# A C table of eight positions in two parts, lag zero as its own products, and added masked scores in a two-layer encoder

## The reference

```python
# S5: a diagonal state-space model, 32 groups of 16 channels, 64 complex states, both directions
bu = einsum('gpc,blgc->blgp', b_bar, u)
states = associative_scan(a_r * a_l, a_r * b_l + b_r)        # over the sequence, forward or reverse
y = einsum('gcp,blgp->blgc', c, states).real                 # summed over both directions, + d * u
...
# GLA: gated linear attention in chunks of 64, four heads, both directions
scores = where(causal_in_chunk, einsum('bnihd,bnjhd->bnhij', q_rel, k_rel), 0.0)
o_intra = einsum('bnhij,bnjhe->bnihe', scores, v)
o_inter = einsum('bnihd,bnhde->bnihe', q * exp(bcum), S_prev)
o = o_intra + o_inter                                        # summed over both directions
```

## Time and profile before

| | |
|---|---|
| time, median of 3 runs | 2458.53 us (2458.19 to 2458.97) |
| the profiled execution | 2458.74 us, of which the span (first to last instruction) is 2457.0 us |
| PE busy | 2420.5 us, 99% |
| DVE busy | 1518.9 us, 62% |
| ACT busy | 1156.1 us, 47% |
| granted TensorE clock, mean | 0.999 of full speed |

### The profile page before, as it was taken

The page is one execution under the profiler, slowest core; times in us unless marked ns, Lnnn a source line. Parts: engine busy times, 40 slices in busy tenths (PEclk is TensorE's granted clock), DMA queues, the critical chain, the costliest instruction groups (busy, mean ns, idle before and its releaser), DMA issues.

```text
span 2457.0 us, 35475 instructions
## 1 busy us (share of the span) xinstructions
PE 2420.5 (99%) x14201; PEld 2065.3 (84%) x14201; DVE 1518.9 (62%) x2570; ACT 1156.1 (47%) x2034; POOL 0.2 (0%) x4
## 2 busy tenths in 40 slices
PE   9999999999999999999999999999999999999999
PEld 5888776778898999898788888888888898888887
DVE  8898757676466755674665447858885554533333
ACT  4333445364444645654453445736764443523432
POOL 0000000000000000000000000000000000000000
PEclk9999999999999999999999999999999999999999
DMA  5435642274223555444224324223234423433232
GB/s 193 107 75 138 218 138 65 78 238 146 86 76 105 181 182 171 120 130 128 78 73 160 112 86 123 92 86 107 92 95 143 132 78 99 133 99 99 95 96 93
DMA packets 110723, 291.34 MB, mean 119 GB/s; under 512 B 18944, under 2 KB 41600, under 8 KB 109280
## 3 DMA queue, kind: packets, MB, share of 16 engines
q1 hardware_dynamic: 99088, 260.38, 33.9%
q10 hardware_dynamic: 11472, 28.71, 3.6%
HBM read 267.45 MB, written 19.50 MB: 117 GB/s over the span
## 4 chain that ended last, share of the span: by engine, by line
PE 82%; DVE 5%; ACT 1%; issue 1%; ACTq 0%; DVEq 0%
PE ps L1455 70%; PE ps L1568 2%; PE ps L1525 2%; PE ps L1550 2%; PE ps L1592 1%; DVE wlo L1432 1%; PE ps L1581 1%; PE ps L1982 1%; DVE ringP L1824 0%; PE ps L1538 0%; PE ps L1992 0%; PE ps L1599 0%; PE ps L1929 0%; PE ps L1469 0%; DVE ps L1748 0%
## 5 line engine op out<-in xcount | busy, mean ns | idle before, releaser
L1427 ACT ACTIVATE whi<-wraw 128x1024 fp32r<-128x1024 f32 x430 | 452.1, 1052 | 188.7 <-PE ps L1455 128.4
L1455 PE MATMUL ps<-in_hP,whi 128*128 128x512 f32 x1336 | 532.5, 399 | 1.6 <-issue 1.6
L1432 DVE TENSOR_TENSOR wlo<-wraw,whi 128x1024 fp32r<-128x1024 f32 x430 | 522.8, 1218 | 3.1 <-ACT whi L1427 2.8
L1455 PE MATMUL ps<-in_hP,wlo 128*128 128x512 f32 x1336 | 520.9, 390 | 0.0
L1455 PE MATMUL ps<-in_lP,whi 128*128 128x512 f32 x1336 | 520.1, 389 | 0.0
L1455 PE MATMUL ps<-in_hS,whi 128*128 128x256 f32 x1088 | 318.0, 292 | 5.6 <-DVE x L1770 4.3
L1455 PE MATMUL ps<-in_lS,whi 128*128 128x256 f32 x1088 | 309.1, 284 | 0.0
L1455 PE MATMUL ps<-in_hS,wlo 128*128 128x256 f32 x1088 | 308.9, 284 | 0.0
L1455 PEld LDWEIGHTS ps<-in_hP,whi 128*128 128x128 f32 x1336 | 250.9, 188 | 59.6 <-issue 8.9
L1455 PEld LDWEIGHTS ps<-in_hP,wlo 128*128 128x128 f32 x1336 | 250.8, 188 | 53.5
L1455 PEld LDWEIGHTS ps<-in_lP,whi 128*128 128x128 f32 x1336 | 251.1, 188 | 51.8 <-issue 1.4
(11 more groups left out here) (486 smaller groups left out, 3671.7 us busy)
## 6 DMA issues: line engine op xcount, KB each, us to landing
wraw<-wt SPq DMA_DIRECT2D x432, 512.0 KB, 3.6
wraw<-wt ACTq DMA_DIRECT2D x17, 512.0 KB, 4.3
k_scratch<-region_P SPq DMA_DIRECT2D x16, 256.0 KB, 3.1
v_scratch<-vtmp SPq DMA_DIRECT2D x32, 128.0 KB, 3.0
x<-x_in SPq DMA_DIRECT2D x4, 768.0 KB, 7.1
mix_mem<-mem_in ACTq DMA_DIRECT2D x1, 2048.0 KB, 15.7
x<-x_in ACTq DMA_DIRECT2D x1, 2048.0 KB, 12.8
region_S<-k_scratch ACTq DMA_DIRECT2D x2, 1024.0 KB, 5.4
```

Of the source, the lines that this page charges most:

```text
L1427: nc.scalar.activation(whi[:, (n + 3) % NHI, :, :], wraw[:, ws(n), :, :], ACT.Copy).then_inc(wh.sem, 1)
L1432: nc.vector.tensor_tensor(wlo[:, ws(n), :, :], wraw[:, ws(n), :, :], whi[:, (n + 3) % NHI, :, :].bitcast(F32), ALU.subtract).then_inc(wr.s ...
L1455: last = nc.tensor.matmul(ps[:, m % 2, 0:N[prod.g]], w_[:, k, :], x_[:, k, :], start=(k == 0 and j == 0), stop=(k == KT - 1 and j == 2))
```

## The change

- `cl` and `qf` have eight positions (lags 1 to 8 for forward, 8 to 1 for reverse) in place of ten. `dve_cl` works on all eight groups at a time, in two parts, real and imaginary: the real part where the first half was, the imaginary part where the second was.
- `pe_lag` makes seven lags (112 columns) per group and direction and places them by group in four column parts of the array (output partitions 0, 32, 64, 96), two groups side by side in a bank: banks 4 and 6. Lag 0 of both directions together is a product of its own: `bbar` by `cc` and by `cneg`, the negated imaginary part (one new DVE instruction, once), 128 rows, 16 columns, into bank 5.
- `act_rt` is eight copies of 16x224 in place of two, and `dve_rt` four additions of 16x32 in place of two of 16x128.
- `pe_bu` waits for each part of `vT` by itself, and writes part 0 to banks 6 and 7, part 1 to 4 and 5.
- In the last block `load_chunks` of group 1 comes after `act_rt` and `load_mt` and before group 2; before, it came ahead of `act_rt`.
- `pe_zeros`, products that nothing reads at the very start, are 33 of 512 columns instead of 25 of 512 and 10 of 256.
- `dve_masks` also adds the two masked scores of a head (two additions per unit), and `pe_heads` multiplies the sum once, for all j first, and then the states. DVE no longer waits there for the unit before.

```diff
-POS = SC + 2
+LAGS = (SC - 1) * GC
...
-                for i in range(15):
-                    nc.tensor.matmul(ps[:, 7, :], w_, x_, start=(i == 0), stop=(i == 14))
-                for i in range(10):
-                    nc.tensor.matmul(ps[:, 6, :], w_, x_, start=(i == 0), stop=False, skip_group_check=True)
-                    nc.tensor.matmul(ps[:, 6, 0:TS], w_, x_[:, 0:TS], start=False, stop=(i == 9), skip_group_check=True)
+                for i in range(33):
+                    nc.tensor.matmul(ps[:, 7, :], w_, x_, start=(i == 0), stop=(i == 32))
...
             def pe_lag(pe, b):
                 pe.wait_ge(cl_ready.sem, b + 1)
                 pe.wait_ge(vt_ready.sem, 2 * b + 2)
-                for g in range(GB):
-                    for z in range(2):
-                        rows = slice(NS * z, NS * z + NS)
-                        lo = 0 if z == 0 else 2
-                        for i in range(2):
-                            last = nc.tensor.matmul(banks(4 + 2 * z, 1024)[0:GC, g * P:(g + 1) * P], bbar[rows, i, GB * b + g, :],
-                                                    cl[rows, i, g, lo:lo + SC, :].rearrange("p n c -> p (n c)"),
+                for e in range(2):
+                    for i in range(2):
+                        for q in range(4):
+                            g = 2 * q + e
+                            for z in range(2):
+                                rows = slice(NS * z, NS * z + NS)
+                                nc.tensor.matmul(ps[32 * q:32 * q + GC, 4 + 2 * z, e * LAGS:(e + 1) * LAGS], bbar[rows, i, GB * b + g, :],
+                                                 cl[rows, i, g, z:z + SC - 1, :].rearrange("p n c -> p (n c)"), start=(i == 0), stop=(i == 1))
+                for e in range(2):
+                    for i, c_ in enumerate((cc[:, 0], cneg)):
+                        for q in range(4):
+                            h = GB * b + 2 * q + e
+                            last = nc.tensor.matmul(ps[32 * q:32 * q + GC, 5, e * GC:(e + 1) * GC], bbar[:, i, h, :], c_[:, h, :],
                                                     start=(i == 0), stop=(i == 1))
                 last.then_inc(lag_done.sem, 1)
...
-                else:
-                    pe.wait_ge(vt_ready.sem, 2 * b + 2)
                 for i in range(2):
+                    pe.wait_ge(vt_ready.sem, 2 * b + i + 1)
                     for g in range(GB):
-                        o = banks(4 + 2 * i, 1024)[:, g * P:g * P + NCH]
+                        o = banks(6 - 2 * i, 1024)[:, g * P:g * P + NCH]
...
-                nc.scalar.activation(rt[:, :, SC:LAG, :], lagf[:, :, 1:SC, :], ACT.Copy)
-                nc.scalar.activation(rt[:, :, 0:SC, :], lagb, ACT.Copy).then_inc(rt_copied.sem, 1)
+                for q in range(4):
+                    nc.scalar.activation(rt[:, 2 * q:2 * q + 2, 0:SC - 1, :], lagb[q], ACT.Copy)
+                    last = nc.scalar.activation(rt[:, 2 * q:2 * q + 2, SC:LAG, :], lagf[q], ACT.Copy)
+                last.then_inc(rt_copied.sem, 1)
...
-            def dve_cl(v, b, halves=(0, 1)):
+            def dve_cl(v, b, parts=(0, 1)):
...
+                for i in parts:
+                    nc.vector.tensor_tensor(cl[:, i], cb[0], qb[i], ALU.mult)
+                    dve_chain(nc.vector.tensor_tensor(tmp, cb[1], qb[1 - i], ALU.mult))
+                    last = nc.vector.tensor_tensor(cl[:, i], cl[:, i], tmp, ALU.subtract if i else ALU.add)
...
             def dve_rt(v, b):
                 v.wait_ge(rt_copied.sem, b + 1)
-                dve_chain(nc.vector.tensor_tensor(rt[:, :, SC - 1, :], rt[:, :, SC - 1, :], lagf[:, :, 0, :], ALU.add))
-                nc.vector.tensor_tensor(rt[:, :, SC - 1, :], rt[:, :, SC - 1, :], dd[:, GB * b:GB * b + GB, :], ALU.add)\
-                    .then_inc(rt_ready.sem, 1)
+                for q in range(4):
+                    last = nc.vector.tensor_tensor(rt[:, 2 * q:2 * q + 2, SC - 1, :], dd[:, GB * b + 2 * q:GB * b + 2 * q + 2, :], lag0[q], ALU.add)
+                last.then_inc(rt_ready.sem, 1)
...
                         tile(t2)
-                        if b == NB - 1:
-                            a.wait_ge(cl_ready.sem, NB)
-                            load_chunks(a, 1)
                         act_rt(a, b)
                         if b == NB - 1:
                             high_tail(a, 0)
                         load_mt(a, b, SC // 2, SC)
                         if b == NB - 1:
+                            load_chunks(a, 1)
                             load_chunks(a, 2)
                         tile(t3)
...
                     for hh in range(2):
                         h = 2 * u.t + hh
-                        for z in range(2):
-                            nc.tensor.matmul(o_ps(hh)[:, js], vtok[u.g][:, j, h * DV:(h + 1) * DV], scT[hh][:, z, js],
-                                             start=(z == 0), stop=False, skip_group_check=True)
+                        nc.tensor.matmul(o_ps(hh)[:, js], vtok[u.g][:, j, h * DV:(h + 1) * DV], u.krel[hh][:, js],
+                                         start=(j == 0), stop=False, skip_group_check=True)
+                for j in range(BL[u.g]):
                     for z in range(2):
...
             def dve_masks(v, u):
                 v.wait_ge(scd.sem, u.i + 1)
-                if u.i > 0:
-                    v.wait_ge(ood.sem, u.i)
...
+                dve_chain(last)
+                for hh in range(2):
+                    last = nc.vector.tensor_tensor(u.krel[hh], scT[hh][:, 0, 0:u.n], scT[hh][:, 1, 0:u.n], ALU.add)
                 last.then_inc(scr.sem, 1)
```

More of the change, by code:

```diff
@@ L492, in act_mem @@
                 nc.scalar.activation(in_hP[:, k, :], mbuf[k % len(mbuf)], ACT.Copy).then_inc(mah.sem, 1)
-            lagf = banks(4, 1024)[0:GC].rearrange("c (g n d) -> c g n d", g=GB, n=SC)
-            lagb = banks(6, 1024)[0:GC].rearrange("c (g n d) -> c g n d", g=GB, n=SC)
+            lagf, lagb = ([ps[32 * q:32 * q + GC, bank_, 0:2 * LAGS].rearrange("c (g n d) -> c g n d", g=2, n=SC - 1) for q in range(4)] for bank_ in (4, 6))
+            lag0 = [ps[32 * q:32 * q + GC, 5, 0:2 * GC].rearrange("c (g d) -> c g d", g=2) for q in range(4)]
             def act_rt(a, b):
@@ L532, in dve_vv @@
                     last.then_inc(t_v.sem, 1)
-            def dve_cl(v, b, halves=(0, 1)):
-                spare = y0 if b == 0 else tmpA[0]
-                tmp = spare[:, 0:4 * POS * GC].rearrange("p (g n c) -> p g n c", g=4, n=POS)
+            def dve_cl(v, b, parts=(0, 1)):
+                spare = sq3[:, :, :].rearrange("p i t -> p (i t)") if b == 0 else tabs
+                tmp = spare[:, 0:GB * P].rearrange("p (g n c) -> p g n c", g=GB, n=SC)
+                hs = slice(GB * b, GB * b + GB)
+                cb = [cc[:, i, hs, :].unsqueeze(2).to_broadcast([P, GB, SC, GC]) for i in range(2)]
+                qb = [qf[:, i, :, hs].rearrange("p n g -> p g n").unsqueeze(3).to_broadcast([P, GB, SC, GC]) for i in range(2)]
                 if b > 0:
                     v.wait_ge(y_done.sem, b)
-                for h in halves:
-                    hs = slice(GB * b + 4 * h, GB * b + 4 * h + 4)
-                    cb = [cc[:, i, hs, :].unsqueeze(2).to_broadcast([P, 4, POS, GC]) for i in range(2)]
-                    qb = [qf[:, i, :, hs].rearrange("p n g -> p g n").unsqueeze(3).to_broadcast([P, 4, POS, GC]) for i in range(2)]
-                    o = [cl[:, i, 4 * h:4 * h + 4] for i in range(2)]
-                    for i, op in ((0, ALU.add), (1, ALU.subtract)):
-                        nc.vector.tensor_tensor(o[i], cb[0], qb[i], ALU.mult)
-                        dve_chain(nc.vector.tensor_tensor(tmp, cb[1], qb[1 - i], ALU.mult))
-                        last = nc.vector.tensor_tensor(o[i], o[i], tmp, op)
-                        if h == 1 and i == 1:
-                            last.then_inc(cl_ready.sem, 1)
-                        else:
-                            dve_chain(last)
+                for i in parts:
+                    nc.vector.tensor_tensor(cl[:, i], cb[0], qb[i], ALU.mult)
+                    dve_chain(nc.vector.tensor_tensor(tmp, cb[1], qb[1 - i], ALU.mult))
+                    last = nc.vector.tensor_tensor(cl[:, i], cl[:, i], tmp, ALU.subtract if i else ALU.add)
+                    if i == 1:
+                        last.then_inc(cl_ready.sem, 1)
+                    else:
+                        dve_chain(last)
             def dve_rot(v, b):
@@ L567, in dve_rt @@
                 v.wait_ge(rt_copied.sem, b + 1)
-                dve_chain(nc.vector.tensor_tensor(rt[:, :, SC - 1, :], rt[:, :, SC - 1, :], lagf[:, :, 0, :], ALU.add))
-                nc.vector.tensor_tensor(rt[:, :, SC - 1, :], rt[:, :, SC - 1, :], dd[:, GB * b:GB * b + GB, :], ALU.add)\
-                    .then_inc(rt_ready.sem, 1)
+                for q in range(4):
```

(5 more changed lines are left out.)

14 lines of the change are left out of this document (7 added, 7 removed).

## The result

The changed kernel takes 2443.0 us (median of 4 runs, 2441.7 to 2445.2) against 2458.75 for the kernel before in the same comparison (4 runs, 2458.2 to 2459.2): ratio 0.9937, 95% interval 0.992 to 0.9954. The forecast was 2443.8. The profiled execution took 2443.60 us, 15.1 less than the 2458.74 of before.

What follows compares the result with a forecast made beforehand. PE's queue of work was taken as the bound (busy 2420.5 of 2457.0 us). 3.6 (state products) + 7.2 (lag products) + 7.5 (GLA) - 3.5 (end of `mixer_in`) = 14.8 us off 2458.7, stated as 2443.8; range 2438.8 to 2449.8.

Steps and rivals of the forecast that it cites:

- Start: `pe_zeros` at the kernel's start: 1,536 more columns, covered by PE's 0.27 us pause; cost 0, at most 0.4 us.
- State products: `pe_bu` in blocks 1 to 3: part 0 starts without waiting for the second `vT` copy; gain 3.6 us, bounds 3.0 and 3.9.
- Lag products: `pe_lag`, four blocks: eight array parts bring 3.61 us a block to 1.8; gain 7.2 us, between 2.0 and 10.4.
- Rival (1): `pe_lag`: instruction starts bind, eight parts no better than four, 2.8 us a block; time 2447.8 us, chance 0.17.
- Copies of `act_rt`: Behind the lag products: eight partly overlapped ACT copies take about 2.8 us for 1.8, so `rt` is ready 1.0 us later.
- End of `mixer_in`: Last block: memory pieces 3 to 5 land later and delay DVE's residues; loss 3.5 us, bounds 1.7 and 4.1.
- its two ways: Last block's delay estimated twice: pieces landing late for DVE, residues at 13.6 to 15.5 for 12.0; ACT's queue 1.9 to 4.0 later.
- Rival (2): Last block: the memory pieces come in time and the 3.5 us loss falls away; time 2440.3 us, chance 0.12.
- GLA heads: `pe_heads`, four units: fewer products and longer runs of one kind; gain 7.5 us, bounds 5.4 and 8.4.
- Rival (4): GLA: ACT and DVE bound the time from unit to unit and eat the gain; time 2451 us, chance 0.06.
- Clock: A 3.4 us half-clock stretch at 533 us costs 1.7 us; one gone, about 2441; one more left out; chance 0.06.
- tail: The loss at the end of `mixer_in` in the last block, put at 3.5 us.

Runs made afterwards that it cites:

- early pieces: The changed kernel, with memory pieces 3 to 5 loaded into a free table (part of the square scratch) ahead of the lag copies: 2438.7 us, ratio 0.9917.
- GLA alone: The kernel before with only the GLA edits (masked scores added, one product with their sum, states in one run, wait dropped): 2450.8 us, ratio 0.9966.
- the run with SP: The changed kernel, but SP issues the loads of memory pieces 3 to 5, behind its own half of `load_mt`: 2445.3 us, ratio 0.9942.
- the run in the old order: The changed kernel, with GLA heads doing `vtok` products then state products for each 128-token tile, masked scores still added: 2446.9 us, ratio 0.9947.

## Why the prediction was right

The place of each effect was right; the sum of 14.8 us stands against 15.1 in the profiles and 15.7 between the medians. Two terms were off by more than a microsecond, in opposite directions.

- **Start**: the pause of 0.27 us is 0.46 now, no cost to be seen, as said.
- **State products**: 3.6 us predicted, 3.6 found, and 4.2 by the run that takes it back.
- **Lag products**: 7.2 predicted, 9.2 found. The term was mis-sized where the block was put at 1.8 us for 1.30. The large products came near the lower end as argued (0.98 us, where scaling by parts gave 0.8, though the price had not halved exactly from two to four parts but gone from 0.056 to 0.030); the small ones were put at the middle of 0.1 and 1.0 and took 0.32. Rival (1), starts that bind, is refuted: 2.8 us a block was its figure. That column parts overlap is shown by the run with neighbours in one part, where only the order differs, and the run with one column part agrees.
- **Copies of `act_rt`**: 2.8 us predicted; from 219.68 to 222.07, 2.4 us.
- **End of `mixer_in`**: a loss of 3.5 predicted, 4.85 found, beyond the upper bound of 4.1. The mechanism was right (the run with early pieces gives 3.8 of it back), its size was off. The working let both loads start when `load_mt` ends and so had them landed at 14.8 at the latest. But DVE waits for both, and `qf` is issued behind `cc`, 1.35 us later, and landed 7.0 us on: 16.2 us after tile 16. Of the miss of the bound, some 1.3 us are this second issue and 0.3 the landing (7.0 for 6.7). With the 1.50 us of the earlier trace rows for the first issue the same sum gives 16.2. The row of a single load was a weak bound too: `bbar` behind `load_mt` landed in 6.7 us before and in 7.9 in the kernel with GLA alone, by the same code. Of its two ways the landing is the one that counts, by the run with SP. Rival (2), pieces in time, is what that kernel with early pieces makes true: it was put at 2440.3 and measures 2438.7.
- **GLA heads**: 7.5 predicted, 8.1 found, inside the bounds. The split was not right: the working has 6.5 us for the 48 records left out (1.09/8 us each) and 1.0 for the longer runs of one kind, and the run in the old order shows 5.4 and 2.7. The cover for DVE's sums held (1.96 us idle). Rival (4) is refuted.
- **Clock**: one more stretch that costs 0.6 us net, which the sum left out, and one that costs nothing. The errors are +2.0 (lag), -1.35 (tail), +0.6 (heads), -0.6 (clock): 0.65 in sum, and so the near hit is in part luck.

## What to carry to other kernels

Short, narrow products are worth spreading over column parts as well as row parts, with neighbours in the queue in different parts: the same 96 records took 4.08, 2.75 or 1.30 us by place and order. Where a change moves several loads behind a busy queue, count to the landing of the last one that the consumer waits for, with the issues ahead of it (1.3 us each here). Then look for memory that is free earlier; here it gave 4.3 us more. Where two chains run to the same end, write down both: shortening one gives only the lead that it has over the other.

## What the hardware showed unasked

- 96 matmul records start in 1.30 us, 13.5 ns apart; the 16-column ones in four column parts start 10 ns apart, and 28 ns in one.
- A 512 KB load landed 4.7 us after its issue on a quiet queue, 6.7 to 8.0 behind four to six other issues of ACT, 7.9 when SP issued it, beside ACT's issues. The issue itself took 0.45 us on the quiet queue and 1.1 to 1.5 right behind `load_mt`.
- One more half-clock stretch of 3.4 us (1.2 GHz) cost 0.6 us net at 428.8, where a later wait gave part of it back, and nothing at 237.7, where DVE was what the end waited for. Which pauses or which kind of work brings one on stays open. Their number differs between executions of one kernel, by the granted clocks beside GLA alone.
